# Four partial sums of the FFN's features: two made ahead of the first up blocks, one behind each of the next two weight splits

## The chip, the cores and the metric

One core of one Trainium2 chip. The metric is the device time of one launch in microseconds (us), the median over runs. The engines are TensorE (PE, matmul), VectorE (DVE), ScalarE (ACT), GpSimd (POOL) and SyncE (SP, which here only issues transfers). Each engine works through its own instruction list in order; they meet only through semaphores.

## The reference

Two layers over x of 512 tokens by 1024 features, in float32. Each has a mixer (a state-space scan in the first, causal pooling in the second) and then a gated MLP, each between two RMS norms. The change touches only the MLP's up projection:

```python
D_MODEL, SEQ, DEPTH, D_FF, FFN_CONV = 1024, 512, 2, 2816, 3

def conv_ffn(u, w_up, conv_w, conv_b, w_down):
    h = u @ w_up.astype(u.dtype)                  # (512, 1024) @ (1024, 5632)
    h = causal_depthwise_conv(h, conv_w, conv_b)  # width 3 along the sequence
    gate, val = jnp.split(h, 2, axis=-1)
    return (jax.nn.silu(gate) * val) @ w_down.astype(u.dtype)

def reference(x, ...):
    for i in range(DEPTH):
        ...
        x = x + rms_norm(mix, norm_mix_post[i])
        f = conv_ffn(rms_norm(x, norm_ffn_pre[i]), w_up[i], conv_w[i], conv_b[i], w_down[i])
        x = x + rms_norm(f, norm_ffn_post[i])
    return x
```

## The kernel before

**Split numbers.** Every float32 operand of a matmul is used as a high and a low part. ACT copies the value to the high part (`split_hi`, L303; `features_act`, L469), DVE subtracts to get the low part (`split_lo`, L309; `features_dve`, L475), and PE makes three passes per product: hi by hi, hi by lo, lo by hi (`three_passes`, L341 to L344).

**Slabs.** The up weights come in slabs of 128 partitions by 2048 elements (1 MB), 22 a layer. Slab S_UP+n lands in `raw[n % 2]`; the load of slab n waits until the slab two earlier has its low part (L300; for a slab that goes through the seven products, the low parts of its weight sums). Iteration i of the up projection (i = 0 to 10) uses two slabs: 2i for two gate blocks (s = 0) and 2i+1 for two value blocks (s = 1). A block is 24 matmuls of 128x512 (`block_product`), so a slab is 48. Each block then goes through the width-3 convolution: ACT does the last tap with the bias (`last_tap`, L560), DVE the other two (`other_taps`, L569, two instructions that wait on each other). ACT takes SiLU of the gate (L1342), DVE multiplies gate by value (L1384).

**The first two iterations and the rest.** Iteration 0 is made block by block while the norm still delivers features (`first_blocks_pe`, L550, 256 columns each). Iteration 1 is plain: 48 matmuls for slab 2, then 48 for slab 3. From iteration 2 on (`SEVEN0 = 2`, nine iterations a layer), the value slab is multiplied by a Strassen-like scheme (`seven_pe`): seven half-size products P1 to P7, 12 matmuls of 128x256 each, instead of eight. It needs four sums of the features and four sums of the slab's weights. The weight sums are made for each slab on DVE (`weights_sum_dve`, L1271 to L1277), split by ACT (L1284) and DVE (L1290). DVE puts the products together in `sevens_dve`.

**The features' sums.** Named `t_sums(1)`, `(2)`, `(4)`, `(3)` in the order in which they are made (`T_ORDER`), 128x1024 each, once a layer. Sum 1 takes three DVE instructions, sum 2 two (it starts from sum 1), sum 4 two (from sum 2), sum 3 three; all are at L1221, each waiting for the one ahead. They lie in `t_new`, which has three places: sum 3 reuses that of sum 1 and so must wait until sum 1 is split. Each is split by one ACT copy (`t_hi`, L1258) and one DVE subtraction (`t_lo`, L1264). PE needs them first in iteration 2: sum 4 in product P4, sum 3 in P7, sums 1 and 2 in P5 and P6.

**What sets the order.** All lists are written out by hand. On DVE, behind the low part of slab 2, stand sums 1, 2 and 4, their three low parts, sum 3, then the taps of iteration 0 (`up_dve(dve, 0, 0)`), its two multiplications, and the low part of slab 3 (in iteration 1), then the taps of iteration 1's gate blocks, the low part of sum 3, the low part of slab 4, the taps of the value blocks, the low part of slab 5 and the first weight sums. On ACT the four copies `t_hi` stand as three ahead of the taps and one behind the SiLUs of iteration 1. PE has no sum work; it waits on `lo_ready` ahead of each slab and, in `seven_pe`, on `t_ready7` (four sums split) ahead of P4 and on `ws_ready` (weight sums split) ahead of P7. Layer 2 has the same lists.

## Time and profile before

| | us |
|---|---|
| median of 3 runs | 1143.71 (1143.59 to 1144.13) |
| the profiled execution | 1143.68 |
| its span, first to last instruction | 1141.8 |
| PE busy | 1118.8 (98%) |
| DVE busy | 859.4 (75%) |
| ACT busy | 565.1 (49%) |
| DVE L1221, 20 sum instructions | about 1.22 each |
| DVE L1264, 8 low parts of sums | about 1.22 each |
| ACT L1258, 8 high parts of sums | about 1.06 each |

A span of 1141.8 us stands for a time of 1143.68 us, so some 1.9 us lie outside of it. The first layer's up projection runs from about 382 to 626 us of the span, the second's from about 772 to 1016 us. In the timeline's rows a merged row gives the start, the time that its instructions took in all, and their count.

### The profile page before, as it was taken

The numbers are of one execution on the slowest core, as the hardware profiler recorded it, in microseconds if no ns is written. First come the engines' busy times: TensorE is split into PE (matmuls) and PEld (weight loads), VectorE is DVE, ScalarE is ACT, GpSimd is POOL, SyncE is SP. The second block draws the span as 40 slices with busy tenths as digits, with TensorE's granted clock in tenths as the row PEclk, the third lists the DMA queues.
The fourth block names the chain that finished last, engine by engine and source line by source line (L and its number), as shares of the span: only waits on it lengthen the run. The fifth ranks groups of instructions, "written<-read, shape, count | busy, mean of one in ns | idle before, by whom it ended". The sixth has DMA issues, their size and how long they took to land.

```text
span 1141.8 us, 15391 instructions
## 1 busy us (share of the span) xinstructions
PE 1118.8 (98%) x6378; PEld 971.7 (85%) x6378; DVE 859.4 (75%) x1011; ACT 565.1 (49%) x650; POOL 37.0 (3%) x93
## 2 busy tenths in 40 slices
PE   8999999999999979999999999999799999999998
PEld 7888888888888968899899888899589989988886
DVE  6778889999754886899998532699789999883235
ACT  5667676767533544444444332574444545532323
POOL 6000000000100000000000000000000000000000
PEclk9999999999999989999999999999899999999999
DMA  8244343433234113323324323512222422323321
GB/s 273 75 136 152 123 130 117 138 117 127 73 111 147 50 64 109 112 74 112 110 74 130 113 90 111 166 37 75 92 75 75 132 89 90 133 75 114 108 74 73
DMA packets 85412, 122.06 MB, mean 107 GB/s; under 512 B 4215, under 2 KB 71391, under 8 KB 85344
## 3 DMA queue, kind: packets, MB, share of 16 engines
q1 hardware_dynamic: 85162, 121.02, 31.9%
q8 instruction: 50, 0.82, 0.3%
q14 instruction: 18, 0.15, 0.0%
q10 hardware_dynamic: 182, 0.07, 0.0%
HBM read 118.92 MB, written 2.16 MB: 106 GB/s over the span
## 4 chain that ended last, share of the span: by engine, by line
PE 92%; DVE 5%; DMA 1%; ACT 1%; issue 1%; DVEq 0%; SPq 0%; ACTq 0%
PE bank L1075 27%; PE bank L342 18%; PE bank L344 18%; PE bank L343 18%; PE bank L550 4%; DVE t_new L1221 2%; PE bank L836 1%; DVE w_lo L312 1%; PE bank L788 1%; PE bank L827 1%; DVE tmp L569 1%; PE bank L778 1%; PE bank L466 1%; PE bank L1447 1%; DMA raw<-in_pool_w 0%
## 5 line engine op out<-in xcount | busy, mean ns | idle before, releaser
L342 PE MATMUL bank<-h_hi,w_hi 128*128 128x512 f32 (+1 forms) x856 | 315.9, 369 | 13.6 <-DVE w_lo L312 13.6
L344 PE MATMUL bank<-h_hi,w_lo 128*128 128x512 f32 (+1 forms) x856 | 312.2, 365 | 0.0
L343 PE MATMUL bank<-h_lo,w_hi 128*128 128x512 f32 (+1 forms) x856 | 312.2, 365 | 0.0
L312 DVE TENSOR_TENSOR w_lo<-raw,w_hi 128x2048 fp32r<-128x2048 f32 x90 | 206.0, 2289 | 17.4 <-ACT w_hi L307 16.2
L307 ACT ACTIVATE w_hi<-raw 128x2048 fp32r<-128x2048 f32 x90 | 171.8, 1909 | 58.4 <-PE bank L344 57.3
L342 PEld LDWEIGHTS bank<-h_hi,w_hi 128*128 128x128 f32 x856 | 162.8, 190 | 39.6 <-DVE w_lo L312 14.4
L344 PEld LDWEIGHTS bank<-h_hi,w_lo 128*128 128x128 f32 x856 | 162.6, 190 | 26.3
L343 PEld LDWEIGHTS bank<-h_lo,w_hi 128*128 128x128 f32 x856 | 162.9, 190 | 24.5
L569 DVE SCALAR_TENSOR_TENSOR tmp<-bank,par,tmp 128x511 f32<-128x511 f32 (+1 forms) x176 | 129.2, 746 | 25.5 <-ACT tmp L560 21.8
L1075 PE MATMUL bank<-w_hi,dn_hi 128*128 128x512 f32 x348 | 107.5, 390 | 0.2 <-DVE w_lo L312 0.2
L1075 PE MATMUL bank<-w_hi,dn_lo 128*128 128x512 f32 x348 | 107.3, 389 | 0.0
L1075 PE MATMUL bank<-w_lo,dn_hi 128*128 128x512 f32 x348 | 107.2, 389 | 0.0
L1427 DVE TENSOR_TENSOR dn_lo<-gated,dn_hi 128x1024 fp32r<-128x1024 f32 x22 | 26.9, 1224 | 105.1 <-ACT dn_hi L1423 105.1
L1284 ACT ACTIVATE w_hi<-raw 128x1024 fp32r<-128x1024 f32 x36 | 36.2, 1052 | 135.2 <-PE bank L344 135.2
L1423 ACT ACTIVATE dn_hi<-gated 128x1024 fp32r<-128x1024 f32 x22 | 23.3, 1058 | 137.6 <-PE bank L1075 137.6
L342 PE MATMUL bank<-t_hi,w_hi 128*128 128x256 f32 x288 | 81.6, 283 | 0.0
L344 PE MATMUL bank<-t_hi,w_lo 128*128 128x256 f32 x288 | 81.6, 283 | 0.0
L343 PE MATMUL bank<-t_lo,w_hi 128*128 128x256 f32 x288 | 81.6, 283 | 0.0
L560 ACT ACTIVATE tmp<-bank,par 128x512 f32<-128x512 f32 x76 | 55.9, 768 | 46.3 <-PE bank L344 35.9
L1075 PEld LDWEIGHTS bank<-w_hi,dn_hi 128*128 128x128 f32 x348 | 65.0, 188 | 14.2 <-DVE w_lo L312 1.0
L1075 PEld LDWEIGHTS bank<-w_hi,dn_lo 128*128 128x128 f32 x348 | 65.3, 188 | 13.6
L1075 PEld LDWEIGHTS bank<-w_lo,dn_hi 128*128 128x128 f32 x348 | 65.4, 188 | 13.6
(228 smaller groups left out, 1608.1 us busy)
## 6 DMA issues: line engine op xcount, KB each, us to landing
raw<-in_ffn_w_up SPq DMA_DIRECT2D x44, 1024.0 KB, 5.0
raw<-in_ffn_w_down SPq DMA_DIRECT2D x22, 1024.0 KB, 4.8
raw<-in_ssd_w_in SPq DMA_DIRECT2D x19, 1024.0 KB, 5.2
decay<-ac_dram SPq DMA_DIRECT2D x16, 512.0 KB, 5.3
raw<-in_ssd_w_out SPq DMA_DIRECT2D x8, 1024.0 KB, 4.9
from_start<-ac_dram SPq DMA_DIRECT2D x32, 128.0 KB, 4.4
xres<-in_x SPq DMA_DIRECT2D x4, 512.0 KB, 5.7
result<-xres SPq DMA_DIRECT2D x3, 512.0 KB, 2.6
```

What stands on the lines that cost most here:

```text
L307: act.activation(w_parts(n)[0][:], raw[n % 2][:], ACT.Copy).then_inc(hi_ready, 1)
L312: dve.tensor_tensor(lo[:], raw[n % 2][:], hi[:].bitcast(F32), ALU.subtract).then_inc(lo_ready, 1)
L342: pe.matmul(dst, wh, xh, start=first, stop=False, **kw)
L343: pe.matmul(dst, wh, xl, start=False, stop=False, **kw)
L344: return pe.matmul(dst, wl, xh, start=False, stop=last, **kw)
L550: mm = pe.matmul(bank[:, 2 * s + j, ts], w[:, k, j * P:(j + 1) * P], x[:, k, ts], start=turn == 0 and k == 0, stop=turn == 2 and k == DB - 1)
L560: act.activation(tmp[:, slot, :], source, ACT.Identity, bias=b, scale=w).then_inc(conv_tap, 1)
L569: dve.scalar_tensor_tensor(tmp[:, slot, back:], source[:, 0:T - back], w, tmp[:, slot, back:], ALU.mult, ALU.add).then_inc(conv_part if j ...
L1075: mm = pe.matmul(bank[:, 2 * c + j, :], x[:, cs(c)], w[:, k, j * T:(j + 1) * T], start=start, stop=stop)
L1284: act.activation(w_hi[1 - w_slot(n)][:, part], raw[n % 2][:, part], ACT.Copy).then_inc(ws_hi_ready, 1)
L1423: act.activation(dn_hi[s % 2][:, :, :], gated[:, 2 * s:2 * s + 2, :], ACT.Copy).then_inc(dn_hi_ready, 1)
L1427: dve.tensor_tensor(dn_lo[s % 2][:, :, :], gated[:, 2 * s:2 * s + 2, :], dn_hi[s % 2][:, :, :].bitcast(F32), ALU.subtract).then_inc(dn_rea ...
```

## The change

The same 20 sum instructions, 8 copies and 8 subtractions are made on the same engines, with the same operands and sizes. `combos_dve` (three sums, then the fourth) becomes `combo_dve`, which makes one sum; `combos_hi_act` and `combos_lo_dve` lose their loops. Ahead of iteration 0's taps DVE now makes sum 1, its low part, sum 2, its low part. Sum 4 and its low part come behind the low part of slab 3 (iteration 1, s = 0). Sum 3 comes behind the low part of slab 4 (s = 1), and its low part between the two value blocks' taps. ACT's copies follow: two ahead of iteration 0's taps, one ahead of iteration 1's gate taps, one between its value taps. PE waits for three split sums ahead of P4, and for the fourth ahead of P7, behind the wait for the first half of the weight sums. The second layer's two hunks, which read as the first's, are left out.

```diff
--- before.py
+++ after.py
@@ -1204,43 +1204,34 @@
                 pe.wait_ge(c_ready, t)
             seven_product(pe, P1, plain(0, 0), h(0, 0))
             seven_product(pe, P2, plain(0, 1), h(1, 0))
-            pe.wait_ge(t_ready7, 4 * (l + 1))
+            pe.wait_ge(t_ready7, 4 * l + 3)
             seven_product(pe, P4, plain(1, 1), combo(4)).then_inc(blk_done, 1)
             pe.wait_ge(ws_ready, 2 * t + 1)
+            pe.wait_ge(t_ready7, 4 * (l + 1))
             seven_product(pe, P7, summed(0, 0), combo(3))
             seven_product(pe, P5, summed(1, 0), combo(1))
             pe.wait_ge(ws_ready, 2 * t + 2)
             seven_product(pe, P6, summed(1, 1), combo(2)).then_inc(p_done, 1)
             seven_product(pe, P3, summed(0, 1), h(1, 1)).then_inc(blk_done, 1)
 
-        def combos_dve(dve, l, last):
-            n = [6 * l]
-
-            def step(out, a, b, op, ready=False):
-                out = out.rearrange("p (k n) -> p k n", n=HALF)
-                ins = dve.tensor_tensor(out, a if a is not None else out, b, op)
-                n[0] += 0 if ready else 1
-                ins.then_inc(t_sum if ready else t_step, 1)
-                dve.wait_ge(*((t_sum, ready) if ready else (t_step, n[0])))
-
+        def combo_dve(dve, l, c):
             hi = lambda k, half: h_part(h_hi, k, half).bitcast(F32)
             lo = lambda k, half: h_part(h_lo, k, half).bitcast(F32)
-            view = lambda ap: ap.rearrange("p (k n) -> p k n", n=HALF)
+            new = lambda j: t_sums(j).rearrange("p (k n) -> p k n", n=HALF)
+            j = T_ORDER[c]
+            first, then = {1: ((hi(0, 1), hi(0, 0)), ((lo(0, 1), ALU.add), (lo(0, 0), ALU.subtract))),
+                           2: ((hi(1, 1), new(1)), ((lo(1, 1), ALU.add),)),
+                           4: ((new(2), hi(1, 0)), ((lo(1, 0), ALU.subtract),)),
+                           3: ((hi(1, 1), hi(0, 1)), ((lo(1, 1), ALU.add), (lo(0, 1), ALU.subtract)))}[j]
+            done = 6 * l + [0, 2, 3, 4][c]
             dve.wait_ge(h_ready, 8 * (1 + 2 * l) + 8)
-            if last:
-                n[0] += 4
+            if j == 3:
                 dve.wait_ge(t_ready7, 4 * l + 1)
-                step(t_sums(3), hi(1, 1), hi(0, 1), ALU.subtract)
-                step(t_sums(3), None, lo(1, 1), ALU.add)
-                step(t_sums(3), None, lo(0, 1), ALU.subtract, 4 * l + 4)
-                return
-            step(t_sums(1), hi(0, 1), hi(0, 0), ALU.subtract)
-            step(t_sums(1), None, lo(0, 1), ALU.add)
-            step(t_sums(1), None, lo(0, 0), ALU.subtract, 4 * l + 1)
-            step(t_sums(2), hi(1, 1), view(t_sums(1)), ALU.subtract)
-            step(t_sums(2), None, lo(1, 1), ALU.add, 4 * l + 2)
-            step(t_sums(4), view(t_sums(2)), hi(1, 0), ALU.subtract)
-            step(t_sums(4), None, lo(1, 0), ALU.subtract, 4 * l + 3)
+            dve.tensor_tensor(new(j), *first, ALU.subtract).then_inc(t_step, 1)
+            for k, (more, op) in enumerate(then):
+                dve.wait_ge(t_step, done + k + 1)
+                dve.tensor_tensor(new(j), new(j), more, op).then_inc(t_sum if k == len(then) - 1 else t_step, 1)
+            dve.wait_ge(t_sum, 4 * l + c + 1)
 
         T_ORDER = [1, 2, 4, 3]
 
@@ -1251,18 +1242,15 @@
         def combo_view(tile, j):
             return tile[:, j - 1, :, :].rearrange("p k n -> p (k n)")
 
-        def combos_hi_act(act, l, turns):
-            for c in turns:
-                j = T_ORDER[c]
-                act.wait_ge(t_sum, 4 * l + c + 1)
-                act.activation(combo_view(t_hi, j), t_sums(j), ACT.Copy).then_inc(t_hi_ready, 1)
-
-        def combos_lo_dve(dve, l, turns):
-            for c in turns:
-                j = T_ORDER[c]
-                dve.wait_ge(t_hi_ready, 4 * l + c + 1)
-                dve.tensor_tensor(combo_view(t_lo, j), t_sums(j), combo_view(t_hi, j).bitcast(F32),
-                                  ALU.subtract).then_inc(t_ready7, 1)
+        def combo_hi_act(act, l, c):
+            act.wait_ge(t_sum, 4 * l + c + 1)
+            act.activation(combo_view(t_hi, T_ORDER[c]), t_sums(T_ORDER[c]), ACT.Copy).then_inc(t_hi_ready, 1)
+
+        def combo_lo_dve(dve, l, c):
+            j = T_ORDER[c]
+            dve.wait_ge(t_hi_ready, 4 * l + c + 1)
+            dve.tensor_tensor(combo_view(t_lo, j), t_sums(j), combo_view(t_hi, j).bitcast(F32),
+                              ALU.subtract).then_inc(t_ready7, 1)
 
         def weights_sum_dve(dve, l, i):
             n, t = S_UP[l] + 2 * i + 1, SEVENS * l + i - SEVEN0
@@ -1348,13 +1336,15 @@
                 for s in range(2):
                     if i:
                         split_hi(act, n + s + 1, (f_done, 4) if l == 0 and i == 1 and s == 0 else (blk_done, base + 2 * s))
+                    if i == SEVEN0 - 1 and s == 0:
+                        combo_hi_act(act, l, 2)
                     for j in range(2):
                         up_tap_act(act, l, i, 2 * s + j)
+                        if i == SEVEN0 - 1 and s == 1 and j == 0:
+                            combo_hi_act(act, l, 3)
                     if s == 0:
                         for j in range(2):
                             up_silu_act(act, l, i, j)
-                    if s == 0 and i == SEVEN0 - 1:
-                        combos_hi_act(act, l, [3])
                 return
             split_hi(act, n + 1, (blk_done, base))
             if i > SEVEN0:
@@ -1389,10 +1379,14 @@
                 for s in range(2):
                     if i:
                         split_lo(dve, n + s + 1)
+                    if i == SEVEN0 - 1:
+                        combo_dve(dve, l, 2 + s)
+                    if i == SEVEN0 - 1 and s == 0:
+                        combo_lo_dve(dve, l, 2)
                     for j in range(2):
                         up_taps_dve(dve, l, i, 2 * s + j)
-                    if s == 0 and i == SEVEN0 - 1:
-                        combos_lo_dve(dve, l, [3])
+                        if i == SEVEN0 - 1 and s == 1 and j == 0:
+                            combo_lo_dve(dve, l, 3)
                 for j in range(2):
                     up_mul_dve(dve, l, i, j)
                 if i == SEVEN0 - 1:
@@ -1726,7 +1720,8 @@
             features_act(act, 1, 2)
             features_act(act, 1, 3)
 
-            combos_hi_act(act, 0, range(3))
+            for c in range(2):
+                combo_hi_act(act, 0, c)
             up_act(act, 0, 0)
             up_act(act, 0, 1)
             for i in range(2, UP_SLABS // 2):
...
@@ -1856,9 +1852,9 @@
             features_dve(dve, 1, 3)
             split_lo(dve, S_UP[0] + 2)
 
-            combos_dve(dve, 0, False)
-            combos_lo_dve(dve, 0, range(3))
-            combos_dve(dve, 0, True)
+            for c in range(2):
+                combo_dve(dve, 0, c)
+                combo_lo_dve(dve, 0, c)
             up_dve(dve, 0, 0)
             up_dve(dve, 0, 1)
             for i in range(2, UP_SLABS // 2):
...
```

DVE, first layer, behind the low part of slab 2, before. `t_new` are sums, `t_lo` their low parts, `tmp` the taps, `gated` iteration 0's multiplications, `w_lo` slab 3:

```order
L1264 TENSOR_TENSOR t_lo<-t_new,t_hi 128x1024 x3
L1221 TENSOR_TENSOR t_new<-h_hi 128x1024
L1221 TENSOR_TENSOR t_new<-t_new,h_lo 128x1024 x2
L569 SCALAR_TENSOR_TENSOR tmp<-bank,par,tmp 128x511
```

```order
L1384 TENSOR_TENSOR gated<-tmp 128x512 x2
L312 TENSOR_TENSOR w_lo<-raw,w_hi 128x2048
L569 SCALAR_TENSOR_TENSOR tmp<-bank,par,tmp 128x511
L569 SCALAR_TENSOR_TENSOR tmp<-bank,par,tmp 128x510
L569 SCALAR_TENSOR_TENSOR tmp<-bank,par,tmp 128x511
L569 SCALAR_TENSOR_TENSOR tmp<-bank,par,tmp 128x510
L1264 TENSOR_TENSOR t_lo<-t_new,t_hi 128x1024
L312 TENSOR_TENSOR w_lo<-raw,w_hi 128x2048
```

The same two places with the change:

```order
L1230 TENSOR_TENSOR t_new<-h_hi,t_new 128x1024
L1233 TENSOR_TENSOR t_new<-t_new,h_lo 128x1024
L1252 TENSOR_TENSOR t_lo<-t_new,t_hi 128x1024
L569 SCALAR_TENSOR_TENSOR tmp<-bank,par,tmp 128x511
```

```order
L1374 TENSOR_TENSOR gated<-tmp 128x512 x2
L312 TENSOR_TENSOR w_lo<-raw,w_hi 128x2048
L1230 TENSOR_TENSOR t_new<-t_new,h_hi 128x1024
L1233 TENSOR_TENSOR t_new<-t_new,h_lo 128x1024
L1252 TENSOR_TENSOR t_lo<-t_new,t_hi 128x1024
L569 SCALAR_TENSOR_TENSOR tmp<-bank,par,tmp 128x511
L569 SCALAR_TENSOR_TENSOR tmp<-bank,par,tmp 128x510
L569 SCALAR_TENSOR_TENSOR tmp<-bank,par,tmp 128x511
L569 SCALAR_TENSOR_TENSOR tmp<-bank,par,tmp 128x510
L312 TENSOR_TENSOR w_lo<-raw,w_hi 128x2048
L1230 TENSOR_TENSOR t_new<-h_hi 128x1024
```

Five sum instructions and one low part have moved from ahead of the first taps to behind the low parts of slabs 3 and 4; the fourth low part, which stood ahead of slab 4, now stands behind it.

ACT, first layer, around iteration 1, before (`w_hi` at L307 is slab 3, then slab 4):

```order
L307 ACTIVATE w_hi<-raw 128x2048
L560 ACTIVATE tmp<-bank,par 128x512 x2
L1342 ACTIVATE tmp<-tmp 128x512 x2
L1258 ACTIVATE t_hi<-t_new 128x1024
L307 ACTIVATE w_hi<-raw 128x2048
L560 ACTIVATE tmp<-bank,par 128x512 x2
```

and with the change:

```order
L307 ACTIVATE w_hi<-raw 128x2048
L1247 ACTIVATE t_hi<-t_new 128x1024
L560 ACTIVATE tmp<-bank,par 128x512 x2
L1330 ACTIVATE tmp<-tmp 128x512 x2
L307 ACTIVATE w_hi<-raw 128x2048
L560 ACTIVATE tmp<-bank,par 128x512
L1247 ACTIVATE t_hi<-t_new 128x1024
L560 ACTIVATE tmp<-bank,par 128x512
```

A copy `t_hi` now stands ahead of the gate taps instead of between the SiLUs and slab 4, and another between the value taps.

## Rows read from the trace of the kernel before

**Rows 1.** The page's first part: busy time and share of the span

```profile
PE 1118.8 (98%) x6378; PEld 971.7 (85%) x6378; DVE 859.4 (75%) x1011; ACT 565.1 (49%) x650; POOL 37.0 (3%) x93
```

**Rows 2.** The waits, whole span: us in total, times, longest

```profile
PE bank L342 <- DVE w_lo L312: 13.6, 2, 7.4
```

**Rows 3.** Timeline of PE, first layer: start, us, what, idle before

```profile
406.61 0.40 PE L342 MATMUL bank<-h_hi,w_hi 128*128 128x512 f32 x1
...
417.30 0.39 PE L344 MATMUL bank<-h_hi,w_lo 128*128 128x512 f32 x1
423.91 0.80 PE L342 MATMUL bank<-h_hi,w_hi 128*128 128x512 f32 x1 [6.23 <-DVE w_lo L312]
...
429.17 0.39 PE L342 MATMUL bank<-h_hi,w_hi 128*128 128x512 f32 x1
```

**Rows 4.** Timeline of PE, second layer

```profile
814.89 0.79 PE L342 MATMUL bank<-h_hi,w_hi 128*128 128x512 f32 x1 [7.36 <-DVE w_lo L312]
...
818.38 0.39 PE L344 MATMUL bank<-h_hi,w_lo 128*128 128x512 f32 x1
```

**Rows 5.** Stretches: us, busy of PE, PEld, DVE, ACT, POOL, granted clock, DMA

```profile
418.00:424.00 6.00, 0.09 (x1) 0.09 (x1) 5.93 (x8) 3.36 (x4) 0.00 (x0) 0.86 0.00 0
424.00:430.00 6.00, 6.00 (x16) 4.74 (x17) 3.90 (x5) 3.85 (x4) 0.00 (x0) 0.57 0.86 307
```

**Rows 6.** Timeline of DVE, first layer

```profile
397.15 1.22 DVE L1221 TENSOR_TENSOR t_new<-h_hi 128x1024 f32<-128x1024 f32 x1
...
400.92 1.23 DVE L1221 TENSOR_TENSOR t_new<-h_hi,t_new 128x1024 f32<-128x1024 f32 x1
...
405.96 3.50 DVE L1264 TENSOR_TENSOR t_lo<-t_new,t_hi 128x1024 fp32r<-128x1024 f32 x3
...
413.14 2.97 DVE L569 SCALAR_TENSOR_TENSOR tmp<-bank,par,tmp 128x511 f32<-128x511 f32 x4
...
421.58 2.28 DVE L312 TENSOR_TENSOR w_lo<-raw,w_hi 128x2048 fp32r<-128x2048 f32 x1
423.78 2.97 DVE L569 SCALAR_TENSOR_TENSOR tmp<-bank,par,tmp 128x511 f32<-128x511 f32 x4
...
430.19 2.29 DVE L312 TENSOR_TENSOR w_lo<-raw,w_hi 128x2048 fp32r<-128x2048 f32 x1 [0.58 <-ACT w_hi L307]
...
439.82 1.28 DVE L1384 TENSOR_TENSOR gated<-tmp 128x512 f32<-128x512 f32 x2
441.02 2.28 DVE L312 TENSOR_TENSOR w_lo<-raw,w_hi 128x2048 fp32r<-128x2048 f32 x1
443.34 0.69 DVE L1271 TENSOR_TENSOR raw<-raw 128x512 f32<-128x512 f32 x1
```

**Rows 7.** Timeline of DVE, second layer: the first taps

```profile
804.12 2.98 DVE L569 SCALAR_TENSOR_TENSOR tmp<-bank,par,tmp 128x511 f32<-128x511 f32 x4
```

**Rows 8.** Timeline of ACT, first layer

```profile
400.92 1.06 ACT L1258 ACTIVATE t_hi<-t_new 128x1024 fp32r<-128x1024 f32 x1 [6.72 <-DVE t_new L1221]
...
408.37 1.28 ACT L1342 ACT_TABLE_LOAD   x1
...
427.31 1.04 ACT L1258 ACTIVATE t_hi<-t_new 128x1024 fp32r<-128x1024 f32 x1
428.26 1.90 ACT L307 ACTIVATE w_hi<-raw 128x2048 fp32r<-128x2048 f32 x1
...
448.44 2.01 ACT L1284 ACTIVATE w_hi<-raw 128x1024 fp32r<-128x1024 f32 x2 [8.29 <-PE bank L344]
```

**Rows 9.** Timeline of DVE, first layer, a later iteration

```profile
470.51 2.36 DVE L1290 TENSOR_TENSOR w_lo<-raw,w_hi 128x1024 fp32r<-128x1024 f32 x2 [0.69 <-ACT w_hi L1284]
...
479.56 0.69 DVE L1307 TENSOR_TENSOR val<-val,bank 128x512 f32<-128x512 f32 x1 [0.75 <-PE bank L344]
...
491.49 2.36 DVE L1290 TENSOR_TENSOR w_lo<-raw,w_hi 128x1024 fp32r<-128x1024 f32 x2 [0.69 <-ACT w_hi L1284]
```

**Rows 10.** The page's DMA issues: KB each, median us to landing

```profile
raw<-in_ffn_w_up SPq DMA_DIRECT2D x44, 1024.0 KB, 5.0
```

More of the change, by code:

```diff
@@ L1767, in _ @@
             split_hi(act, S_UP[1] + 2)
-            combos_hi_act(act, 1, range(3))
+            for c in range(2):
+                combo_hi_act(act, 1, c)
             up_act(act, 1, 0)
@@ L1857, in _ @@
             split_lo(dve, S_UP[0] + 2)
-            combos_dve(dve, 0, False)
-            combos_lo_dve(dve, 0, range(3))
-            combos_dve(dve, 0, True)
+            for c in range(2):
+                combo_dve(dve, 0, c)
+                combo_lo_dve(dve, 0, c)
             up_dve(dve, 0, 0)
@@ L1901, in _ @@
             split_lo(dve, S_UP[1] + 2)
-            combos_dve(dve, 1, False)
-            combos_lo_dve(dve, 1, range(3))
-            combos_dve(dve, 1, True)
+            for c in range(2):
+                combo_dve(dve, 1, c)
+                combo_lo_dve(dve, 1, c)
             up_dve(dve, 1, 0)
```

## The prediction

> **What bounds the kernel now.** Read the busy shares first: PE works 98% of the span [rows 1]. So only two things can be won: PE's own work, which the change leaves as it is, and the time in which PE waits or runs slowly. The waits name them: in the whole span PE waits twice for DVE's low part of a weight slab, 13.6 us together [rows 2]. The timelines of PE show where: 6.23 us at 423.91 and 7.36 us at 814.89, each time ahead of slab 3, the value slab of iteration 1 [rows 3, 4]. Behind each wait PE is slow for a while. A slab of 48 matmuls starts its first and its last at 406.61 and 417.30, so one takes 0.227 us and the slab 10.92 us. From 423.91 to 429.17 only 12 matmuls start, 2.5 us more than at that pace; from 814.89 to 818.38 only 8, 1.7 us more [rows 3, 4]. The stretches show why: the granted clock is 0.86 in the idle stretch and 0.57 just behind it, so mostly the lower of the two levels, 1.2 GHz [rows 5]. The two stalls cost 13.6 + 4.2 = 17.8 us. They end when DVE has made slab 3's low part, and DVE, from 397.15 to 423.8, is busy nearly without a gap, so its list is the bound there [rows 6].
>
> **Ahead of the first taps.** A sum instruction, which waits for the one ahead of it, takes a place of 1.26 us (three from 397.15 to 400.92); a low part that waits for nothing new 1.14 us (three in 3.50, the last one 1.22) [rows 6]. Leaving that place: sum 4, two instructions, 2.51; sum 3, three, 3.77; sum 4's low part, 1.14. Together 7.42 us. Entering it: in the old list each sum's ACT copy ran beside the next sum on DVE; now DVE needs the copy right away, twice. A copy takes 1.06 us [rows 8], with some 0.04 us for the semaphore 1.10; twice, 2.20 us. The taps start 7.42 - 2.20 = 5.22 us earlier: at 407.92 instead of 413.14 [rows 6], in layer 2 at 798.90 instead of 804.12 [rows 7].
>
> From the first tap to PE's resuming are 10.77 us in both layers (413.14 to 423.91, 804.12 to 814.89) [rows 3, 4, 6, 7]. Nothing in this piece of the lists changes. One cover thins: ACT's table load of 1.28 us at 408.37 [rows 8] can come 0.2 us earlier only and ends at about 409.45, just when the first SiLU is due (1.5 us behind the first tap). I count it as hidden; uncovered it costs 0.1 to 0.3 us a layer. PE resumes at 418.69 and 809.67. It had run dry at 417.68 and 807.53 (the start less the wait), so the waits shrink to 1.0 and 2.1 us.
>
> **Slab 4, a new wait.** Behind slab 3's low part, whose place is 2.20 us (421.58 to 423.78) [rows 6], DVE now has sum 4 (2.51), the wait for its copy (1.10) and its low part (1.14), 4.75 us. The gate taps of iteration 1 start at 423.78 - 5.22 + 4.75 = 423.31, only 0.47 us earlier than before. ACT has its copy of sum 4 ahead of these taps instead of behind the SiLUs, which takes 0.95 us (427.31 to 428.26) from the way to slab 4 [rows 8]. Slab 4's low part, started at 430.19 before, starts at 430.19 - 0.47 - 0.95 = 428.77 and ends at 431.06, 2.29 us later [rows 6]. PE, resumed at 418.69 at full clock, is through slab 3 at 429.61 and waits until 431.1, 1.5 us. This wait did not exist before: PE was then busy until 437.4.
>
> **Slab 5.** DVE goes on at 430.97 with sum 3 (3.77), the two value taps (2.95, half of it on either side of a low part of 1.14), and two multiplications (1.20, 439.82 to 441.02) [rows 6]; that is 9.06 us, so slab 5's low part starts at 440.03 and ends at 442.3. ACT's copies there (sum 3's beside DVE's first value tap) are in time. PE is through slab 4 at 431.1 + 10.92 = 442.0: a wait of 0.3 us.
>
> **Slab 6.** An iteration from the third on takes 20.98 us (470.51 to 491.49) [rows 9], of which the seven products take 20.98 - 10.92 = 10.06. DVE adds the four weight sums (2.9 us from 442.36, at 0.69 and a semaphore each), two low parts (2.36 [rows 9]), four tap instructions (2.95) and slab 6's low part (2.29): done at 452.75. ACT's copy of slab 6 waits for P4, which ends three products (4.3 us) into the seven, and fits. PE arrives at 442.35 + 10.06 = 452.4: a wait of 0.4 us. Sum 4 and sum 3 are ready long before P4 and P7, so PE's two `t_ready7` waits cost nothing. Slab 7's load is issued behind the weight sums' low parts at 447.6 and lands 5.0 us later [rows 10], within 0.1 us of the moment when ACT may copy it; DVE wants that copy some 3 us later.
>
> **The sum.** Iteration 3's first block started at 423.91 + 5.26 + 36 x 0.227 + 10.92 + 10.06 = 458.3 before, and starts at 452.8 now: 5.5 us. In layer 2 it was 814.89 + 3.49 + 40 x 0.227 + 20.98 = 848.4, and is 452.8 + (809.67 - 418.69) = 843.8: 4.7 us, because the slow stretch that goes is shorter. Together 10.2 us. From there nothing is late: DVE is idle 0.69 + 0.75 us in each later iteration [rows 9], so its lag, some 0.4 us against PE, is made up in one.
>
> This holds at full clock. If PE is still slow behind the wait ahead of slab 3, the loss falls mostly into the wait ahead of slab 4: in layer 1 slab 3 ends at 432.1 instead of 429.6, and at iteration 3 0.3 us of the 2.5 are left; in layer 2 none of the 1.7. I take 10.1 us. The profiled execution, 1143.68, and the median, 1143.71, are the same for this, so the forecast is 1143.7 - 10.1 = 1133.6 us.
>
> **Rivals.**
>
> *The clock falls at the new short waits as well.* The trace has no wait of 1 to 2 us in these stages to read from; the nearest are those of 6.23 and 7.36 us, which brought 2.5 and 1.7 us of slow running [rows 3, 4]. Behind the wait ahead of slab 4 such a loss has only the 0.3 and 0.4 us of the next two waits to fall into, so it costs 1.0 to 1.8 us a layer, 2.0 to 3.6 together: 1135.6 to 1137.2. Against it: in the idle stretch of 6 us the clock was still 0.86 on average [rows 5], so it stayed up for most of it. The Trainium skill (TensorE: Matmul & The Clock Gate, section HAM oscillation) speaks for this rival: waits between short bursts can throw the array back to half rate each time, and it is this that a change which turns one long wait into four short ones invites. By that rule the time would be the upper end, 1137; no row here shows it either way. 14%.
>
> *DVE's lag stays in the loop.* Before, DVE started each iteration from PE's signal with its work done; now it starts late. If its idle 1.44 us cannot be used, because it sits behind signals that still come from PE (copies behind P4, products behind P6), PE waits some 0.4 us in each of 8 more iterations a layer: 16 x 0.4 = 6.4 us of the gain is gone, 1140.0. Against: P4's copy and slab 6's low part need 4.3 + 0.2 + 1.9 + 2.3 = 8.7 us of the 10.06. 6%.
>
> *The same mechanism, slower than before.* If that wait is above 10.1 / 16 = 0.63 us an iteration, the gain is eaten; at 1.0 us the time is 1143.7 + 5.9 = 1149.6. It would need DVE's list for an iteration to take 21.6 us, where the rows leave 20.98 - 1.44 = 19.5. 3%.
>
> *The stall ahead of slab 3 is ended by something else.* If slab 3's load or ACT's copy were late too, DVE's shorter list would win nothing: 1143.7. The load needs only slab 1's low part, made before 397, and 5.0 us [rows 10]. 2%.
>
> *More than the sum*, above 12 us, if ACT's copies overlap DVE better than counted: 3%.
>
> **Chances and range.** The forecast has the remaining 72%; its own range is 1132.5 to 1135.0, from terms a few tenths off in six places. With the clock's rival the range is 1132.3 to 1137.3, which leaves out about 15%. A measurement can tell about 0.2%, 2.3 us, from no change. Faster by more than that: 72 + 14 + 3 and most of the second rival, 94%; within it 3%; slower 3%.
>
> **What would show it.** In the profile after: waits of PE ahead of slab 3 of 1.0 and 2.1 us, ahead of slab 4 of 1.5 us or less, ahead of slabs 5 and 6 below 0.5 us, and none later; DVE idle 1.1 us twice ahead of the first taps, which start at 407.9; iteration 3's block at 452.8 and 843.8; later iterations of 20.98 us. Wrong would be: a granted clock below 1 behind slab 4's wait (first rival), waits in iterations beyond the fourth (second and third), or a wait above 3 us ahead of slab 3 (fourth).

## The result and the profile after

| | before | changed |
|---|---|---|
| median, us | 1143.92 (4 runs, 1143.59 to 1144.38) | 1134.84 (4 runs, 1134.53 to 1135.08) |
| ratio | | 0.9922, interval 0.9906 to 0.9938 |
| the profiled execution, us | 1143.68 | 1134.63 |
| its span, us | 1141.8 | 1132.9 |

The changed kernel is 9.1 us faster. 10.1 were forecast (1133.6 us), so the forecast is 1.2 us low and inside its range. The first part of the page after, and the waits of PE from 300 us to the end (us in total, times, longest), which answer to [rows 1, 2]:

```profile
PE 1118.2 (99%) x6378; PEld 969.3 (86%) x6378; DVE 858.4 (76%) x1011; ACT 565.1 (50%) x650; POOL 38.2 (3%) x93
```

```profile
PE bank L342 <- DVE w_lo L312: 4.7, 3, 2.2
PE bank L1075 <- DVE w_lo L312: 0.2, 1, 0.2
```

No engine's busy time has moved by more than some 1 us. What has gone is PE's wait for slabs: 4.7 us where it was 13.6, in three pieces instead of two. The timeline of PE shows the pieces, and the first matmul of iteration 3 in each layer (the rows without a wait); these answer to [rows 3, 4]:

```profile
418.67 0.50 PE L342 MATMUL bank<-h_hi,w_hi 128*128 128x512 f32 x1 [1.13 <-DVE w_lo L312]
...
431.17 0.50 PE L342 MATMUL bank<-h_hi,w_hi 128*128 128x512 f32 x1 [1.32 <-DVE w_lo L312]
...
452.71 0.50 PE L342 MATMUL bank<-h_hi,w_hi 128*128 128x512 f32 x1
```

```profile
804.31 0.50 PE L342 MATMUL bank<-h_hi,w_hi 128*128 128x512 f32 x1 [2.25 <-DVE w_lo L312]
...
838.35 0.50 PE L342 MATMUL bank<-h_hi,w_hi 128*128 128x512 f32 x1
```

In layer 1 there is a wait ahead of slab 3 and a new one ahead of slab 4. In layer 2 there is only the first, and 816.92, where slab 4 starts, shows none. The next fence tells why. It holds stretches of the same execution (columns as in [rows 5]), before and behind the wait in each layer:

```profile
417.00:419.00 2.00, 0.87 (x4) 0.42 (x3) 2.00 (x2) 0.00 (x0) 0.00 (x0) 1.00 0.00 0
419.00:422.00 3.00, 3.00 (x15) 2.46 (x14) 1.98 (x2) 0.95 (x1) 0.00 (x0) 1.00 0.71 233
...
802.00:805.00 3.00, 0.75 (x4) 0.61 (x4) 3.00 (x3) 0.00 (x0) 0.00 (x0) 1.00 0.00 0
805.00:808.00 3.00, 3.00 (x10) 2.28 (x9) 1.77 (x3) 1.32 (x2) 0.00 (x0) 0.54 0.85 272
```

Behind the wait in layer 1 the granted clock is 1.00. Behind the 2.25 us wait in layer 2 it is 0.54, so mostly 1.2 GHz, and 10 matmuls run in 3 us where 15 do at full clock. Slab 3 ends later by about what PE would have waited ahead of slab 4: a second execution, below, starts slab 4 at 816.81, with a wait and at full clock.

The timeline of DVE, first layer, answers to [rows 6]:

```profile
397.00 1.22 DVE L1230 TENSOR_TENSOR t_new<-h_hi 128x1024 f32<-128x1024 f32 x1
398.26 2.49 DVE L1233 TENSOR_TENSOR t_new<-t_new,h_lo 128x1024 f32<-128x1024 f32 x2
401.94 1.23 DVE L1252 TENSOR_TENSOR t_lo<-t_new,t_hi 128x1024 fp32r<-128x1024 f32 x1 [1.20 <-ACT t_hi L1247]
...
406.76 1.23 DVE L1252 TENSOR_TENSOR t_lo<-t_new,t_hi 128x1024 fp32r<-128x1024 f32 x1 [1.20 <-ACT t_hi L1247]
407.90 2.97 DVE L569 SCALAR_TENSOR_TENSOR tmp<-bank,par,tmp 128x511 f32<-128x511 f32 x4
...
422.21 1.23 DVE L1252 TENSOR_TENSOR t_lo<-t_new,t_hi 128x1024 fp32r<-128x1024 f32 x1 [1.20 <-ACT t_hi L1247]
423.35 2.97 DVE L569 SCALAR_TENSOR_TENSOR tmp<-bank,par,tmp 128x511 f32<-128x511 f32 x4
428.82 2.29 DVE L312 TENSOR_TENSOR w_lo<-raw,w_hi 128x2048 fp32r<-128x2048 f32 x1 [2.50 <-ACT w_hi L307]
...
440.03 2.28 DVE L312 TENSOR_TENSOR w_lo<-raw,w_hi 128x2048 fp32r<-128x2048 f32 x1
```

The price of the new order is plain here: DVE sits idle for 1.20 us at each of the three copies it now needs at once. The first taps start at 407.90 instead of 413.14, and the first sum at 397.00 instead of 397.15, which is ahead of anything that the change touches.

**Where the time lies.** Three marks cut the execution: DVE's first sum in layer 1, its first sum in layer 2, and its last instruction (L399). Before: 397.15, 788.13, 1137.94. Changed: 397.00, 782.65, 1127.94. So 5.33 us come in layer 1, 4.52 in layer 2, 0.15 ahead of both: 10.0 at the last vector instruction. From its start to the end of the span there are 3.9 us before (1141.8 - 1137.94) and 5.0 now (1132.9 - 1127.94). This takes 1.1 us back, far from anything the change touches, and leaves the 8.9 us by which the span is shorter. The three marks are used for each kernel below, since a time of a whole run mixes the parts. Near its start DVE's first copy of a weight slab waits for its load, 0.15 us here and 1.48 in `e1` and 1.00 in `e3`, and so moves the first sum (397.98 and 397.89 there) without any edit at that place.

How exact are the marks? The kernel before, profiled a second time (`e8`), takes 390.42 and 349.54 us for the two layers where the first trace has 390.98 and 349.81. The difference lies behind the two long waits: slab 4 starts 12.94 and 12.33 us behind slab 3 instead of 13.45 and 12.59, so the slow stretch itself differs in length by 0.3 to 0.5 us. Against this second trace the change gains 9.0 us up to the last vector instruction, against the first 9.85 in the two layers.

### The profile page after: what moved, and what is told of

It reads as the page before. It is cut to its first block, busy times and chain, and to the rows that moved or that the text cites. A ratio compares the mean times of both kernels' runs of the same rounds, so it can differ in the third digit from the quotient of the medians.

```text
span 1132.9 us, 15413 instructions
## 1 busy us (share of the span) xinstructions
PE 1118.2 (99%) x6378; PEld 969.3 (86%) x6378; DVE 858.4 (76%) x1011; ACT 565.1 (50%) x650; POOL 38.2 (3%) x93
## 4 chain that ended last, share of the span: by engine, by line
PE 91%; DVE 5%; ACT 2%; DMA 1%; issue 1%; DVEq 0%; ACTq 0%
PE bank L1075 27%; PE bank L342 17%; PE bank L344 17%; PE bank L343 17%; PE bank L550 4%; PE bank L836 1%; DVE w_lo L312 1%; DVE tmp L569 1%; PE bank L788 1%; PE bank L827 1%; PE bank L778 1%; DVE t_new L1233 1%; PE bank L466 1%; PE bank L1441 1%; DVE t_lo L1252 1%
## 5 line engine op out<-in xcount | busy, mean ns | idle before, releaser
L342 PE MATMUL bank<-h_hi,w_hi 128*128 128x512 f32 (+1 forms) x856 | 315.0, 368 | 4.8 <-DVE w_lo L312 4.7
L307 ACT ACTIVATE w_hi<-raw 128x2048 fp32r<-128x2048 f32 x90 | 171.9, 1910 | 54.5 <-PE bank L344 53.4
L342 PEld LDWEIGHTS bank<-h_hi,w_hi 128*128 128x128 f32 x856 | 162.1, 189 | 32.4 <-DVE w_lo L312 7.3
L342 PE MATMUL bank<-t_hi,w_hi 128*128 128x256 f32 x288 | 81.5, 283 | 0.0
L1075 PEld LDWEIGHTS bank<-w_lo,dn_hi 128*128 128x128 f32 x348 | 65.3, 188 | 13.6
```

The lines of the kernel that those rows point to most:

```text
L307: act.activation(w_parts(n)[0][:], raw[n % 2][:], ACT.Copy).then_inc(hi_ready, 1)
L342: pe.matmul(dst, wh, xh, start=first, stop=False, **kw)
L1075: mm = pe.matmul(bank[:, 2 * c + j, :], x[:, cs(c)], w[:, k, j * T:(j + 1) * T], start=start, stop=stop)
```

## The experiments

**Theory**: the gain is the sum of the prediction. DVE's list ahead of slab 3 bounds, a slow stretch in front of the new wait is swallowed by it, and nothing is late from iteration 3 on. **Rivals**: the slow clock costs time of its own; DVE's slack in later iterations is smaller than counted. A later question was the 1.1 us at the end.

### One layer at a time

`e1` has the new order in layer 1 and the old one in layer 2, `e2` the reverse. In layer 2 of `e1` this stands (and its ACT and DVE lists in `up_act` and `up_dve` keep the old places there):

```diff
-            for c in range(2):
+            for c in range(3):
                 combo_dve(dve, 1, c)
+            for c in range(3):
                 combo_lo_dve(dve, 1, c)
+            combo_dve(dve, 1, 3)
```

> The first layer has the changed lists, the second those of before. Theory (DVE's list ahead of slab 3 is the bound, layer by layer): the waits ahead of slab 3 are 1.1 us in layer 1 and again 7.4 us in layer 2; iteration 3 of layer 1 starts 5.5 us earlier, and nothing of that is lost up to the last vector instruction; time 1143.9 - 5.5 = 1138.4, plus up to 1.1 us where the last store lands late as in the changed kernel. Rival (the lag is given back later in the layer): less than 4 us, with waits of PE in later iterations.

> Only the second layer has the changed lists. Theory: the wait in layer 1 stays 6.2 us with 12 slow matmuls, that of layer 2 is 2.2 us at full clock; 4.6 us less, 1139.3, again plus up to 1.1 us at the last store. Together with the run of layer 1 alone the two gains must add up to the changed kernel's 10.0 us at the last vector instruction. Rival (the two layers' gains are not independent): the sum is off by over 1 us.

Measured: `e1` 1140.32 us (1139.76 to 1140.74), ratio 0.9964 (0.9951 to 0.9977); `e2` 1140.21 (1139.76 to 1140.51), 0.9961 (0.9946 to 0.9975). With the late end counted in, 1139.5 and 1140.4 were expected: `e1` is 0.8 us above it (its first sum comes 1 us late, see above, and the kernel before measured 1144.39 beside it instead of 1143.9), `e2` within. By the marks layer 1 of `e1` is 5.27 us shorter and layer 2 of `e2` 4.49, the untouched layers within 0.4 of the first trace of before. The halves of the gain are independent and add up to the whole, less the end, where both have 5.0 us. The timeline of PE in layer 2 of `e2` gives more:

```profile
809.94 0.50 PE L342 MATMUL bank<-h_hi,w_hi 128*128 128x512 f32 x1 [2.27 <-DVE w_lo L312]
...
822.44 0.50 PE L342 MATMUL bank<-h_hi,w_hi 128*128 128x512 f32 x1 [1.33 <-DVE w_lo L312]
```

The same code as in the changed kernel, the same first wait, but here the clock stayed up and the wait of slab 4 is there. From the first sum to the last vector instruction layer 2 takes 345.32 us with the clock up and took 345.29 with the clock down. The changed kernel, profiled once more (`e9`, below), gives the same pair inside one program: at 804.31 the same 2.25 us wait, granted clock 1.00 behind it, 1.33 us ahead of slab 4, and iteration 3 at 838.35 again. The stretch of `e9` that answers to the one with 0.54 above, and its first matmul of slab 4:

```profile
805.00:808.00 3.00, 3.00 (x15) 2.47 (x14) 1.77 (x3) 1.32 (x2) 0.00 (x0) 1.00 0.84 272
```

```profile
816.81 0.50 PE L342 MATMUL bank<-h_hi,w_hi 128*128 128x512 f32 x1 [1.33 <-DVE w_lo L312]
```

So at this place the slow stretch and the wait of slab 4 stand in for each other, and the swallowing is shown. `e7`, below, shows a place where it fails.

### What a slow stretch costs without a wait behind it

`e3` moves sum 3 alone. Sums 1, 2 and 4 with their low parts stand ahead of the first taps, without an exposed copy, and sum 3 goes behind slab 4's low part as in the change. DVE's part of the edit (ACT's copies follow):

```diff
-                    if i == SEVEN0 - 1:
-                        combo_dve(dve, l, 2 + s)
-                    if i == SEVEN0 - 1 and s == 0:
-                        combo_lo_dve(dve, l, 2)
+                    if i == SEVEN0 - 1 and s == 1:
+                        combo_dve(dve, l, 3)
...
-            for c in range(2):
+            for c in range(3):
                 combo_dve(dve, 0, c)
+            for c in range(3):
                 combo_lo_dve(dve, 0, c)
```

> Only sum 3 is moved behind slab 4's low part (its low part between the value taps); sums 1, 2 and 4 stay ahead of the first taps, as three sums and then three low parts, so no ACT copy is exposed. DVE's first taps start 3.77 us earlier instead of 5.22: waits ahead of slab 3 of 2.5 and 3.6 us, and no new wait ahead of slab 4, 5 or 6. If the clock stays up through such waits, layer 1 gains 6.2 and layer 2 5.3 us, 11.5 together, more than the full change: 1132.4 to 1133.5. If it falls as behind the waits of 6.2 and 7.4 us (2.5 and 1.7 us each), 3.8 + 3.8 = 7.5: 1136.4 to 1137.5. The rival that sum 4's place matters more than the exposed copies predicts at most the changed kernel's 10.0.

Measured: 1136.76 us (1134.61 to 1137.65, 4 runs), ratio 0.9929 (0.9914 to 0.9944). The timeline of PE in both layers, and stretches behind its waits:

```profile
420.89 0.50 PE L342 MATMUL bank<-h_hi,w_hi 128*128 128x512 f32 x1 [2.46 <-DVE w_lo L312]
...
807.29 0.79 PE L342 MATMUL bank<-h_hi,w_hi 128*128 128x512 f32 x1 [3.61 <-DVE w_lo L312]
```

```profile
421.00:424.00 3.00, 3.00 (x8) 2.37 (x9) 2.65 (x4) 0.88 (x2) 0.00 (x0) 0.56 0.67 201
807.00:810.00 3.00, 2.71 (x6) 2.15 (x7) 2.93 (x5) 0.63 (x1) 0.00 (x0) 0.51 0.52 143
```

Both waits are 3.8 us shorter than before, which is sum 3's place of 3.77. By the marks the layers gain 4.58 and 3.87, so only 0.8 and 0.1 us of the 2.5 and 1.7 us of slow running are won back. A slow stretch thus still costs some 1.6 us a layer when no wait stands behind it (from slab 3's first matmul to slab 4's are 12.60 and 12.51 us, against 11.0 at full clock). That is the price which the first rival named; in the changed kernel the wait ahead of slab 4 pays it. One of the four runs, at 1134.61, has a granted clock of 0.997 over the whole, as the changed kernel's execution with one slow stretch has; the other three have 0.994 or 0.995. This suggests, and no trace shows, that only one stretch was slow in it. Since the clock fell, `e3` can't tell the price of sum 4's place from that of the exposed copies. The next two kernels do.

### The exposed copies, and the wait of slab 4

`e4` makes sums 1 and 2 and then both low parts, so that each copy runs beside a vector instruction again. `e5` does this too and takes sum 4's copy and low part from ahead of the gate taps to behind them. The edit of `e5` (that of `e4` is its last three lines, and the same in layer 2):

```diff
-                    if i == SEVEN0 - 1 and s == 0:
-                        combo_hi_act(act, l, 2)
                     for j in range(2):
                         up_tap_act(act, l, i, 2 * s + j)
...
+                    if i == SEVEN0 - 1 and s == 0:
+                        combo_hi_act(act, l, 2)
...
-                    if i == SEVEN0 - 1 and s == 0:
-                        combo_lo_dve(dve, l, 2)
                     for j in range(2):
                         up_taps_dve(dve, l, i, 2 * s + j)
...
+                    if i == SEVEN0 - 1 and s == 0:
+                        combo_lo_dve(dve, l, 2)
...
                 combo_dve(dve, 0, c)
+            for c in range(2):
                 combo_lo_dve(dve, 0, c)
```

> As the changed kernel, but ahead of the first taps DVE makes sums 1 and 2 and then their two low parts, so that ACT's two copies run beside DVE's work. Theory (each exposed copy costs DVE 1.2 us, and DVE is the bound): first taps 2.3 us earlier than in the changed kernel; the wait ahead of slab 3 is gone in layer 1 (PE is through slab 2 only at 417.5) and under 0.2 us in layer 2; ahead of slab 4 0.4 and 1.4 us, slabs 5 and 6 0.3 each as before; gain over the changed kernel 2.2 us a layer, 4.4 together, 1130.4. Rival (the new bound sits behind slab 3, in sum 4 and its copy ahead of the gate taps, so that earlier first taps only lengthen the wait ahead of slab 4): under 1 us.

> As the run with sums 1 and 2 paired, and in iteration 1 ACT's copy of sum 4 stands behind the two gate taps and DVE's low part of it behind its gate taps, so that no copy is exposed anywhere. Theory (each exposed copy, and DVE's idle time ahead of slab 4's low part, is on the path): slab 4's low part comes 2.3 us earlier than in the paired kernel, all of PE's waits ahead of slabs 3 to 6 go; 0.9 us more in layer 1 and 2.0 us in layer 2, 2.9 together: 1127.3 against 1130.2. Rival (slab 4's wait turns into one ahead of slab 5 or 6, since DVE's sum of work is unchanged): under 1 us, with waits of over 0.5 us there.

Measured: `e4` 1130.24 us (1130.05 to 1130.48), ratio 0.9875 (0.9860 to 0.9890); `e5` 1126.86 (1126.78 to 1126.94), 0.9847 (0.9831 to 0.9863). The timeline of DVE in `e5`, first layer:

```profile
403.53 2.36 DVE L1252 TENSOR_TENSOR t_lo<-t_new,t_hi 128x1024 fp32r<-128x1024 f32 x2
405.81 2.97 DVE L569 SCALAR_TENSOR_TENSOR tmp<-bank,par,tmp 128x511 f32<-128x511 f32 x4
...
414.24 2.28 DVE L312 TENSOR_TENSOR w_lo<-raw,w_hi 128x2048 fp32r<-128x2048 f32 x1
...
424.43 2.29 DVE L312 TENSOR_TENSOR w_lo<-raw,w_hi 128x2048 fp32r<-128x2048 f32 x1 [1.37 <-ACT w_hi L307]
```

In `e5` the two low parts stand back to back, the taps start 2.3 us earlier from the first sum on (8.57 us instead of 10.90), and slab 3's low part is done before PE wants it. `e4` still waits ahead of slab 4, 0.42 us in layer 1 and 1.33 in layer 2; in `e5` no matmul of L342 waits in either layer. By the marks `e4` is 4.5 us shorter than the changed kernel (4.4 expected), and `e5` 3.6 shorter than `e4` (2.9 expected): from slab 4's first matmul to iteration 3's in layer 1 are 20.95 us instead of 21.55, since small delays of PE at slabs 5 and 6 went as well. By the marks `e5` gains 8.93 and 9.00 us, 17.9 together. The prediction put the cost of both stalls at 17.8 [rows 2 to 4]: this checks that term by itself, and shows that 8 of the 18 us were left by the change. (Against the second trace of before, whose slow stretches are shorter, it is 17.1.)

### How much slack the later iterations have

`e6` adds one vector instruction of 128x1024 to each iteration from the third on, 18 in all, and `e7` two. They take the maximum of a value with itself, in place:

```diff
             weights_lo_dve(dve, l, i)
+            for e in range(1):
+                dve.tensor_tensor(xres[:, e, :], xres[:, e, :], xres[:, e, :], ALU.max)
```

> The changed kernel with one more DVE instruction of 128x1024 (the maximum of a residual row with itself, 1.14 us of DVE's list, result unchanged) in each iteration from the third on, 18 in all. Theory (DVE has 1.44 us to spare in an iteration, and a lag is made up there): DVE's list becomes 20.7 us against PE's 20.98, so only the first such iteration of each layer shows it, the wait ahead of slab 6 growing from 0.3 to 1.4 us, and 0.3 us more where the first down part is split: 2.9 us slower than the changed kernel, 1137.7. Rival (the lag is kept, DVE's idle time cannot be used): 18 x 1.14 = 20.5 us slower, 1155.

> Two such instructions in each iteration. Theory: DVE's list is now 21.8 us, 0.9 us over PE's, so PE waits 0.9 us in every one of the iterations, on top of 2.6 us in the first: about 9.5 us a layer, 19 us together over the changed kernel, 1153.8. This is slower than the kernel before, and shows the price of the rival in which DVE's lag stays in the loop. Rival (DVE can fit more beside PE than counted): under 8 us.

Measured: `e6` 1137.25 us (2 runs), ratio 0.9938 (0.9918 to 0.9958); `e7` 1158.41 (2 runs), 1.0123 (1.0102 to 1.0143). The waits of PE in `e6`, then in `e7`, from 300 us on, and the timeline of PE in `e7`:

```profile
PE bank L342 <- DVE w_lo L312: 8.3, 6, 2.3
```

```profile
PE bank L342 <- DVE w_lo L312: 22.9, 20, 2.3
```

```profile
477.24 0.50 PE L342 MATMUL bank<-h_hi,w_hi 128*128 128x512 f32 x1 [0.83 <-DVE w_lo L312]
499.32 0.50 PE L342 MATMUL bank<-h_hi,w_hi 128*128 128x512 f32 x1 [0.83 <-DVE w_lo L312]
```

One instruction costs 1.14 us of wait ahead of slab 6 in each layer: in the changed kernel that low part ends just as PE comes, so there is no slack at this place. From there on the period is 20.98 us again, with two exceptions. In each layer another 0.34 us come at the start of iteration 6, behind the place where DVE splits the first down part too (0.3 were expected), and in layer 1 the wait in the down projection is 0.93 us instead of 0.24. By the marks `e6` is 3.7 us longer than the changed kernel, not the 2.9 expected. The time of the whole run came out right (1137.25 for 1137.7) only because this kernel has the short end, 1.1 us less. That hit is luck.

Two make DVE the bound: the period is 22.08 us (477.24 to 499.32) instead of 20.98. Of the added 2 x 1.14 = 2.28 us, 1.10 shows and 1.18 was slack. The 1.10 can be read from PE's rows. Ahead of 477.24 the last product matmul starts at 476.13, so at its pace of 0.12 us the next is due at 476.25 and comes 0.99 late (the listed 0.83 counts from that matmul's end), and behind the wait the second matmul starts some 0.33 us after the first instead of 0.23. So the third rival's mechanism exists, and at +1.10 us an iteration it does end slower than before; its condition does not hold by 1.18 us in each iteration.

`e7` came out 4.6 us above what was expected of it, and by the marks 24.8 us above the changed kernel where 19 were expected, again with the short end. The expectation had 0.9 us an iteration for 1.10, since it took the idle time of [rows 9] in a lump and had no price for PE's restart. Another 1.6 us are a slow stretch. Layer 1 grew by 11.58 us, layer 2 by 13.19. The rows show PE in layer 2, the stretch of 4 us behind the wait at 852.37 (columns as in [rows 5]), DVE in the same iteration, and DVE at the same place in layer 1:

```profile
852.37 0.50 PE L342 MATMUL bank<-h_hi,w_hi 128*128 128x512 f32 x1 [2.29 <-DVE w_lo L312]
...
876.06 0.50 PE L342 MATMUL bank<-h_hi,w_hi 128*128 128x512 f32 x1 [0.83 <-DVE w_lo L312]
```

```profile
852.37:856.37 4.00, 4.00 (x11) 3.13 (x12) 3.90 (x5) 1.74 (x3) 0.00 (x0) 0.57 0.73 236
```

```profile
866.28 2.36 DVE L1278 TENSOR_TENSOR w_lo<-raw,w_hi 128x1024 fp32r<-128x1024 f32 x2 [2.27 <-ACT w_hi L1272]
```

```profile
467.47 2.36 DVE L1278 TENSOR_TENSOR w_lo<-raw,w_hi 128x1024 fp32r<-128x1024 f32 x2 [0.67 <-ACT w_hi L1272]
```

The clock fell behind a wait of 2.29 us, and this iteration takes 23.69 us instead of 22.08. The next wait is 0.83 us as everywhere, so nothing was swallowed, though a wait for DVE stands right behind. The reason is in DVE's rows: its low parts of the weight sums wait for ACT, ACT's copies there wait for PE (8.82 us instead of 7.22), and so PE's lateness comes back to PE. Ahead of slab 4 in the changed kernel DVE's work did not wait for the slow PE (the low part starts at 814.46 in both executions, with the slow stretch and without), and there the loss was swallowed.

### The 1.1 us at the end

Kernels by what they have from the start of the last vector instruction to the end of the span: before, the repeat of before (`e8`), `e6` and `e7` 3.9 us; changed and `e1` to `e5` 5.0. That is neither the order of the sums nor the speed. The program's instruction count sorts them: 15391 in both of before, 15431 in `e6` and 15449 in `e7`, and 15413 in all six with the long end.

> The kernel before, unchanged, for a second trace. Two intervals differ between the traces so far with no edit at that place: DVE's first copy of a weight slab waits 0.15 or 1.48 us for its load near the start, and the last store lands 2.0 or 3.1 us after it is issued. If these belong to the execution and not to the program, this trace may show either in other values than the first one did (0.18 and 2.0), while the two waits of 6.2 and 7.4 us stay. If the late landing belongs to the changed programs, it is 2.0 again.

`e8` gave 1142.88 us in its one run, the two waits again (6.23 and 7.35 us) and the short end. To tell length from the rest, `e10` is the changed kernel with 18 vector instructions of one column, which take next to no time but make it 15431 long, and `e11` is `e5` with the same:

```diff
             weights_lo_dve(dve, l, i)
+            for e in range(1):
+                dve.tensor_tensor(xres[:, e, 0:1], xres[:, e, 0:1], xres[:, e, 0:1], ALU.max)
```

> The changed kernel, once more, as the neighbour of the next kernel on the same chip. Both theories of its end expect what its first profile had: 1134.5 to 1135.1 us, a last store of 3.1 us, and 5.0 us from the start of the last vector instruction to the end of the span.

> The changed kernel with one vector instruction of one column (a maximum of a value with itself) behind the low part of each later up iteration, 18 in all: nearly no time (by the small vector instructions of these traces below 0.1 us each, in idle time of the vector engine) but as many more instructions as the kernel with one large instruction had. Theory 1, a program of this length has no instruction load in its last 14 us: the last store takes 2.6 us or less, 3.9 us from the last vector instruction's start to the end, 1133.7 us. Theory 2, the long last store belongs to something else in the order of the work: 5.0 us at the end and 1134.8 us. Theory 3, the kernel with the large instructions had the short end because its work was late there: also 5.0 us and 1134.8 us.

> The kernel with the pair of sums ahead and the third low part late, with the same 18 small vector instructions. Theory 1: no instruction load in the last 14 us, 3.9 us from the last vector instruction's start to the end and 1125.8 us. Theories 2 and 3: 5.0 us there, and 1126.9 us as without them.

Measured on one chip: `e9` 1135.15 us (1134.67 to 1135.39, 5 runs), ratio 0.9921 (0.9907 to 0.9935); `e10` 1134.10 (1133.81 to 1134.77, 4 runs), 0.9913 (0.9899 to 0.9926); `e11` 1125.70 (1125.44 to 1125.96, 4 runs), 0.9838 (0.9825 to 0.9852). The time from the issue of a store of the result to its landing (least, median, longest) in `e9`'s twin, the changed kernel as first profiled, then in `e10`:

```profile
DMA to landing us min/median/max: 2.0/2.6/3.1
```

```profile
DMA to landing us min/median/max: 2.0/2.6/2.6
```

The transfers in the last 3 us of `e9`, by queue (packets, MB, share of 16 engines), then in those of `e10`:

```profile
q1 hardware_dynamic: 211, 0.37, 33.5%
q14 instruction: 1, 0.01, 0.6%
```

```profile
q1 hardware_dynamic: 288, 0.52, 48.3%
```

With 18 more instructions the kernel is 1.05 us faster by the medians, and `e11` is 1.16 us faster than `e5` (measured beside other runs of before, 1143.85 against 1144.31, so 0.7 by that comparison; in the traces the end is 1.1 us shorter). The end is 3.9 us in both. The queue of instruction loads moves one packet in the last 3 us of `e9`, none in the last 14 of `e10`, whose last one lies over 100 us ahead of the end. All seven traces of 15413 instructions have that packet, a longest store of 3.1 us and the long end; none of the other six has any of the three. Theory 1 stands. Shown is that the long end and the late load go with the number of instructions and not with the work. Whether it is the number in all or where a load's border falls in one engine's list is not separated, and how the load lengthens the store, on a shared engine or otherwise, is not shown.

## Why the prediction was right, step by step

| step | forecast | measured |
|---|---|---|
| exposed copy, each | 1.10 us | 1.17 (1.20 idle) |
| first taps, layer 1, from its first sum | 10.77 | 10.90 |
| wait ahead of slab 3, layers 1 and 2 | 1.0, 2.1 | 1.13, 2.25 |
| gate taps, then slab 4's low part, from the first sum | 26.16, 31.62 | 26.35, 31.82 |
| slab 4: PE late by | 1.5 | 1.48 (listed as a wait of 1.32) |
| slab 5's low part, from the first sum; PE late by | 42.88; 0.3 | 43.03; 0.18 |
| slab 6: PE late by | 0.4 | 0.16 |
| iteration 3, layer 1, from its first sum | 55.65 | 55.71 |
| iteration 3, layer 2, from its first sum | 55.7 | 55.70 |
| gain up to the last vector instruction | 10.1 | 10.0, 0.15 of it ahead of both layers |
| later iterations | 20.98 | 20.98 (the first 21.09) |
| the time | 1133.6 | 1134.84 |

The forecast's times are on the clock of before, where the first sums are at 397.15 and 788.13; in the changed kernel they are at 397.00 and 782.65, so the distance from the first sum is what compares. The forecast's 407.92 for the first taps and the measured 407.90 look like a fit to 0.02, but 0.15 us of this is the earlier first sum; the step itself was 0.13 us too short. The same holds for the other times of layer 1.

**Ahead of the first taps** the working was the right kind: a place on DVE per instruction, and one whole copy for each sum whose low part follows at once. The copy was sized 0.07 us too small: 401.94 - 397.00 = 4.94 us for three sum instructions of 1.26 and the copy leave it 1.17. The low part behind it took its 1.14.

**The table load**, the cover that thinned, held. ACT's timeline has it from 408.01, done in time for the SiLU at 409.47, which waited for DVE:

```profile
408.01 1.28 ACT L1330 ACT_TABLE_LOAD   x1
409.47 0.63 ACT L1330 ACTIVATE tmp<-tmp 128x512 f32<-128x512 f32 x1 [0.17 <-DVE tmp L569]
```

**The new wait ahead of slab 4** was forecast by going on with the same count past the place that the change was about; it is there, at 1.32 us. The small waits at slabs 5 and 6 are too short to be listed, but PE starts these slabs 0.18 and 0.16 us later than its pace has it due (442.37 for 442.19, 452.71 for 452.55). The forecast had no price for PE's restart behind a wait, some 0.1 us each time, and its waits here were too long by about as much, so that iteration 3 fits to 0.06: in part the errors cancelled. `e6` shows how thin this was: any further work on DVE ahead of slab 6 is on the path at once.

**The clock.** The forecast said that a slow stretch behind slab 3's wait falls into slab 4's and that layer 2 would keep none of it. This is what happened, and `e2` and `e9` show the same wait without the slow stretch, at the same length of the layer. Why the clock falls in one execution and not in the next no run here explains; the swallowing made it not matter. The traces bear out the clock rival's price (1.6 us in each layer of `e3` and once in `e7`) but not its place: behind waits of 1.1 to 1.4 us no profiled execution shows a clock below 1, and of the eight waits of 2.24 to 2.29 us in all traces two have one below 1 behind them, one of them in the changed kernel, whose second trace has not. The Trainium skill (TensorE: Matmul & The Clock Gate, section HAM oscillation) tells of a kernel in which the wait behind each short burst throws the array back to half rate. Its waits are about 3 to 5 us long, longer than any new one here, so the prediction stretched that case when it took its upper end from it; the measured clock decides, and here the waits up to 1.4 us cost nothing of the kind.

**The lag in the loop.** From iteration 4 on the period is 20.98 us and no later iteration waits. `e7` measures the slack at 1.18 us an iteration. The prediction counted 1.44, which holds 0.69 us that DVE spends on ACT's copy and cannot use (0.67 of it are still idle in `e7`, at 467.47). The 0.75 us that is left makes up most of the 1.18; the other 0.4 must lie in gaps that are too short to be listed, which I did not trace.

**What was missed** is the end: the sum had no term for the 1.1 us by which the last store is late, and could have had none from the trace of before, whose last 3 us show no instruction load. With it the forecast would have stood at 1134.7 for 1134.84. That is closer than the parts allow: the change is worth 9.0 or 9.85 us by the marks, by the trace of before that one takes, and the changed kernel at the length of `e10` is 9.75 us below its neighbours of before in the medians, some 0.2 less than it would be without the eighteen small instructions (by the marks 731.13 us from the first sum to the last vector instruction, 730.95 without). The forecast of 10.1 stands 0.1 to 1.1 us above these.

**The better version** is `e11`: pairs of sums with their low parts behind, the third low part behind the gate taps, and a length that keeps the instruction load away from the end, 1125.7 us, 18 us below before. It also shows what the change paid for making the sums singly: each sum that is split at once costs DVE 1.2 us of waiting for ACT.

## What to carry to other kernels

When work moves out of a stall, go on counting past the stall to the place where the two engines agree again: here the new wait was one slab on, and it decided both the gain and whether the slow clock cost anything. But count on a wait to swallow a delay only where the work that it waits for does not itself wait for the delayed engine: in `e7` it did, and 1.6 us were lost in full. Keep a vector instruction between a producer and the subtraction that needs its copy on another engine; two sums and then two low parts are worth 2.3 us against sum, low, sum, low. For differences of about 1 us compare stretches between marks inside the program, not whole times, since the end can move by that much with the mere count of instructions.

## What the runs showed of the hardware

- The granted clock fell to 0.54 behind a wait of 2.25 us in one execution of the changed kernel and stayed at 1.00 behind the same wait in another. In all traces it fell behind two of eight waits of 2.24 to 2.29 us, behind those of 2.46 and 3.61 us in `e3`, and behind none of the waits up to 1.4 us. Such a stretch costs some 1.6 us where nothing swallows it.
- A program of 15413 instructions ends 1.1 us later than its neighbours of 15391, 15431 and 15449, with one packet of the instruction queue in its last 3 us and a longest store of 3.1 us instead of 2.6.
- Behind a wait PE's second matmul of 128x512 starts 0.33 us after the first instead of 0.23.
- An exchange from DVE to an ACT copy of 128x1024 and back leaves DVE idle for 1.20 us, of which the copy itself is 1.06.
